# Two-layer block in fp32 pairs: shared weight buffers (7 and 4), and eight stage changes made by halves of the tokens

## The reference

```python
def rmsnorm(x, g):
    y = x * rsqrt(mean(x * x, axis=-1) + EPS)          # per token, over the 1024 channels
    return y * g

# first block, before each mixer and each FFN
h = rms_norm(x, g) * (1 + scale) + shift
x = x + gate * stage(h)                                # stage: w_in ... w_out, or gate/up/down

# second block, six times
hn = rmsnorm(x, pre_g) * (1 + scale) + shift
y = rmsnorm(fn(hn), post_g)
x = x + res_w * gate * y
```

## Time and profile before

| | us |
|---|---|
| median of 3 runs | 3777.99 (3772.76 to 3780.68) |
| the profiled execution's own time | 3780.26 |
| its span | 3778.2 |
| TensorE matmul busy | 3590.5 (95%) |
| VectorE busy | 2017.1 (53%) |
| ScalarE busy | 1333.3 (35%) |
| mean granted TensorE clock | 0.969 |
| DMA | 429.06 MB, 114 GB/s |

### The profile page before, as it was taken

How to read it: one execution, slowest core, us unless ns; L and a number is a source line. 1 busy time by engine, 2 the same in 40 slices (tenths; PEclk the granted TensorE clock), 3 DMA queues, 4 the chain that set the end, 5 groups by cost and what they waited for, 6 DMA issues and landing times.

```text
span 3778.2 us, 41003 instructions
## 1 busy us (share of the span) xinstructions
PE 3590.5 (95%) x16372; PEld 2854.7 (76%) x16372; DVE 2017.1 (53%) x3608; ACT 1333.3 (35%) x2291; POOL 127.9 (3%) x126
## 2 busy tenths in 40 slices
PE   5889999999999999998999999999999999979998
PEld 4647888766788788876677888788878888868886
DVE  7856756676766664456765235523553333344234
ACT  3563323344323332234443223322323334333232
POOL 3330000000000000000100000000000000000000
PEclk9999999989999999999999999999999999989999
DMA  6214554422455545422012222222222222212221
GB/s 250 101 40 162 191 197 165 177 80 90 163 201 184 188 178 198 154 67 75 23 51 78 100 96 95 83 96 95 101 77 83 73 79 86 66 51 95 100 95 62
DMA packets 155466, 429.06 MB, mean 114 GB/s; under 512 B 45467, under 2 KB 50523, under 8 KB 155276
## 3 DMA queue, kind: packets, MB, share of 16 engines
q1 hardware_dynamic: 155276, 426.45, 32.5%
HBM read 423.98 MB, written 2.40 MB: 113 GB/s over the span
## 4 chain that ended last, share of the span: by engine, by line
PE 83%; DVE 11%; ACT 3%; issue 1%; DMA 1%; POOL 0%; SPq 0%; ACTq 0%; DVEq 0%; POOLq 0%
PE ps L412 24%; PE ps L414 24%; PE ps L413 24%; PE ps L711 1%; PE ps L449 1%; PE ps L456 1%; DVE TT L1515 1%; DVE wlo L1448 1%; DVE HL L1500 1%; PE ps L751 1%; PE ps L789 1%; DVE X L1601 1%; PE ps L776 1%; PE ps L557 1%; PE ps L570 1%
## 5 line engine op out<-in xcount | busy, mean ns | idle before, releaser
L412 PE MATMUL ps<-HH,whi 128*128 128x512 f32 x3168 | 1262.7, 399 | 49.9 <-DVE HL L1500 27.8
L413 PE MATMUL ps<-HL,whi 128*128 128x512 f32 x3168 | 1243.8, 393 | 0.0
L414 PE MATMUL ps<-HH,wlo 128*128 128x512 f32 x3168 | 1243.6, 393 | 0.0
L1448 DVE TENSOR_TENSOR wlo<-wraw,whi 128x1024 fp32r<-128x1024 f32 x526 | 644.0, 1225 | 787.3 <-ACT whi L914 787.1
L914 ACT ACTIVATE whi<-wraw 128x1024 fp32r<-128x1024 f32 x548 | 576.3, 1054 | 697.4 <-PE ps L414 685.2
L412 PEld LDWEIGHTS ps<-HH,whi 128*128 128x128 f32 x3168 | 601.8, 190 | 207.4 <-issue 65.0
L413 PEld LDWEIGHTS ps<-HL,whi 128*128 128x128 f32 x3168 | 602.0, 190 | 127.4 <-issue 4.6
L414 PEld LDWEIGHTS ps<-HH,wlo 128*128 128x128 f32 x3168 | 601.0, 190 | 128.1
L1436 DVE CUSTOM_DVE_ANT_0 mraw<-mraw,CB 128x1024 f32<-128x1024 f32 x224 | 282.5, 1262 | 0.6 <-DMA mraw<-mst 0.5
L1634 DVE TENSOR_TENSOR TT<-TT,ps 128x512 f32<-128x512 f32 x116 | 79.7, 687 | 216.9 <-PE ps L414 187.6
L412 PE MATMUL ps<-PHf,whi 128*128 128x512 f32 x352 | 136.9, 389 | 0.0
(11 more groups left out here) (325 smaller groups left out, 3844.1 us busy)
## 6 DMA issues: line engine op xcount, KB each, us to landing
wraw<-wst SPq DMA_DIRECT2D x548, 512.0 KB, 3.7
mraw<-mst SPq DMA_DIRECT2D x224, 512.0 KB, 3.4
MR<-mst SPq DMA_DIRECT2D x16, 512.0 KB, 13.8
X<-xt SPq DMA_DIRECT2D x8, 256.0 KB, 5.1
BB<-bvec SPq DMA_DIRECT2D x8, 256.0 KB, 4.5
TT<-lse SPq DMA_DIRECT2D x16, 128.0 KB, 3.1
out<-X SPq DMA_DIRECT2D x8, 256.0 KB, 2.0
CB<-crow SPq DMA_DIRECT2D x2, 512.0 KB, 4.2
```

The lines of the kernel that those rows point to most:

```text
L412: e.matmul(o[key], wh, sh(k), start=k == 0, stop=False)
L413: e.matmul(o[key], wh, sl(k), start=False, stop=False)
L414: ins = e.matmul(o[key], wl, sh(k), start=False, stop=k == nk - 1)
L1448: e.tensor_tensor(wlo[:, x % SPLIT, :], wraw[:, x % RAW, :], whi[:, x % SPLIT, :].bitcast(F32), ALU.subtract).then_inc(*wlo_made.up(x))
```

## The change

**Buffers.** RAW is 7, SPLIT 4, and wlo has no buffer of its own: it is written over wraw of the same block. So `load(b)` waits for ("w", b - RAW) in place of the wlo of that block, and whi of a block is free one block later. SyncE's steps in `dilated()` are moved to fit, and the six first projections of mla become 4 and 2.

**Halves.** In the eight stage changes the last outputs (from m = 5 with out_proj, from 6 with a down-projection) are made first for tokens 0 to 255 and then for 256 to 511, with 256-column matmuls in a pass over the same weights each (`proj_halves`, `end_halves`); so are the first four projections (`begin_halves`). Sums, root, spread and modulation are made for each half. The sums and spread of the first half stand among the matmuls of the second pass of the outputs, those of the second half among the first pass of the projections. ("w", b) is signalled in the second pass alone. `seam` (ScalarE), `single_seam` and `double_seam` (VectorE) give the order of the rest, `fed_late` the places of the last three feeds. The norms after dilated(), the first norm and the last stay as they were.

```diff
-RAW, SPLIT = 5, 3
+RAW, SPLIT = 7, 4
...
-    gs = [(8, [("mla_in", i) for i in range(6)])]
+    gs = [(8, [("mla_in", i) for i in range(4)]), (8, [("mla_in", i) for i in (4, 5)])]
...
+        raw_off = pos[0]
         wraw = sb("wraw", [P, RAW, BT * 128])
+        wlo = at("wlo", raw_off, [P, RAW, BT * 128], F32R)
         whi = sb("whi", [P, SPLIT, BT * 128], F32R)
-        wlo = sb("wlo", [P, SPLIT, BT * 128], F32R)
...
+        split_at = {("f", 0, 1): 5, ("f", 1, 0): 6, ("f", 1, 1): 5, ("p", 0, 0): 6,
+                    ("q", 0, 0): 6, ("q", 0, 1): 5, ("q", 0, 2): 6, ("q", 1, 0): 6}
...
+            def proj_halves(order, nk, sh, sl, ready, apart, hook):
+                first = lane.tile
+                for hf in (0, 1):
+                    lane.tile = first
+                    cs = slice(256 * hf, 256 * hf + 256)
+                    for n, (key, k) in enumerate(order):
+                        wh, wl, names = weights(1)
+                        own = key + (hf,) if apart else key
+                        if k == 0 and (apart or hf == 0):
+                            take(own, apart[hf] if apart else main[0])
+                        o = ps[:, bank_of[own], cs]
+                        lane.wait_ge(*ready(k, hf))
+                        e.matmul(o, wh, sh(k)[:, cs], start=k == 0, stop=False, skip_group_check=True)
+                        e.matmul(o, wh, sl(k)[:, cs], start=False, stop=False, skip_group_check=True)
+                        ins = e.matmul(o, wl, sh(k)[:, cs], start=False, stop=k == nk - 1, skip_group_check=True)
+                        up = names if hf else []
+                        if k == nk - 1:
+                            up = up + ([own] if apart else []) + ([key] if hf else [])
+                        if up:
+                            ins.then_inc(*mm_done.up(*up))
+                        hook(hf, n)
...
+            def end_halves(s, keys, nk, sh, sl, ready):
+                sa, order = halves_of(s)[0], [(key, k) for key in keys for k in range(nk)]
+
+                def hook(hf, n):
+                    if hf and n == (5 if s[0] == "q" else 4):
+                        half_total(sa)
+                    elif hf and n == (len(order) - 1 if s[0] == "q" else 11):
+                        half_spread(sa)
+
+                proj_halves(order, nk, sh, sl, lambda k, hf: ready(k), (Ring(0, 1, 2), Ring(*((3, 0, 7) if len(keys) == 3 else (2, 7)))),
...
+
+                def hook(hf, n):
+                    if not hf and n == 7:
+                        half_total(sb)
+                    elif not hf and n == 23:
+                        half_spread(sb)
+
+                main[0] = Ring(0, 1, 2, 3)
+                proj_halves([(key, k) for k in range(8) for key in keys], 8, hh, hl, lambda k, hf: (v_norm, ("hl", z + (hf,), k)), None,
+                            hook)
...
+            def modulate_half(s, v, last_read, beside):
...
+                for m in range(8):
+                    lane.wait_ge(v_norm, ("b", s, m))
+                    e.activation(HH[:, m, cs], T[m % 5][:, cs], ACT.Identity, bias=MOD[:, v, m:m + 1]).then_inc(
+                        *a_norm.up(("hh", s, m)))
+                    beside(m)
+
+            def fed_late(m):
+                if m in (3, 5, 7):
+                    feed(8)
+
...
+            def modulate_half(s, v, idx, beside, prior=None, update=None):
...
+                for m in range(8):
+                    if m >= 5:
+                        lane.wait_ge(v_norm, ("hl", s, m - 5))
+                    if update is not None:
+                        lane.wait_ge(v_norm, ("x", prior, m))
+                    e.scalar_tensor_tensor(T[m % 5][:, cs], X[:, m, cs], AM[:, idx, m:m + 1], R, ALU.mult, ALU.mult).then_inc(
+                        *v_norm.up(("b", s, m)))
+                    if update is not None and m < 7:
+                        update(m + 1)
+                    if update is not None:
+                        lowered(m)
+                    elif m:
+                        lowered(m - 1)
+                    beside(m)
+                if update is None:
+                    lowered(7)
...
+            def single_seam(s, key, gate, nk):
...
+                square_add(s, first - 1)
+                if nk == 8:
+                    feed(8)
+                for m in range(first, 8):
+                    update(sa, m)
+                single(sa)
+                feed(nk)
+                for m in range(first, 7):
+                    update(sb, m)
+
+                def beside(m):
+                    if m == 0:
+                        feed(nk)
+                    elif m == 3:
+                        update(sb, 7)
+                        feed(8)
+                    elif m == 5:
+                        single_half(sb)
+                    elif m == 6:
+                        single_root(sb)
+
+                modulate_half(sa, v, idx, beside)
+                modulate_half(sb, v, idx, fed_late)
...
+            def double_seam(s, stage, nk):
...
+                square_add(s, first - 1)
+                gained_add(s, first - 1)
+                if nk == 8:
+                    feed(8)
+                for m in range(first, 8):
+                    output(sa, m)
+                first_half(sa)
+                roots(sa)
+                feed(nk)
+                for m in range(first, 7):
+                    output(sb, m)
+                rsqrt(za, 4)
+                diagonal(za, 4, T[2])
+
+                def beside(m):
+                    if m == 0:
+                        feed(nk)
+                    elif m == 1:
+                        output(sb, 7)
+                    elif m == 2:
+                        first_half(sb)
+                    elif m == 3:
+                        roots(sb)
+                    elif m == 4:
+                        feed(8)
+                    elif m == 5:
+                        rsqrt(zb, 4)
+                        diagonal(zb, 4, T[2])
+
+                modulate_half(za, v, nxt, beside, sa, updater(sa))
+                modulate_half(zb, v, nxt, fed_late, sb, updater(sb))
...
             def load(b):
                 if b < nblocks:
                     if b >= RAW:
-                        lane.wait_ge(lo_signal(b - RAW), b - RAW)
+                        lane.wait_ge(mm_done, ("w", b - RAW))
...
                     for n in range(9):
-                        if c < 7 or n < 4:
+                        if c < 7 or 5 <= n < 8:
                             feed(8)
-                        if n == 1 and c:
-                            totals(c - 1)
-                        elif n == 2 and c:
+                        if n == 2 and c:
                             inverses(c - 1)
-                        elif n == 5:
+                        elif n == 3:
                             maxima(c)
-                        elif n == 6:
+                        elif n == 4:
                             tops(c)
-                totals(7)
+                        elif n == 8:
+                            totals(c)
                 inverses(7)
```

More of the change, by code:

```diff
@@ L402, in weights @@
                 last = o + n == BT or lane.tile == len(tiles)
-                return whi[:, b % SPLIT, sl], wlo[:, b % SPLIT, sl], [("w", b)] if last else []
+                return whi[:, b % SPLIT, sl], wlo[:, b % RAW, sl], [("w", b)] if last else []
             def proj(keys, nk, sh, sl, ready, between=None, ks=None):
@@ L464, in norm_total, with half_sums @@
                 spread(s, next_bank)
[L466 to L470, removed]
+            def half_sums(s, o, src, rhs, at_, first=False):
+                for j in range(2 * s[3], 2 * s[3] + 2):
+                    ins = e.matmul(o[:, 4 * j + at_:4 * j + at_ + rhs.shape[1]], src[:, 128 * j:128 * j + 128], rhs,
+                                   start=first and j == 2 * s[3], stop=j == 2 * s[3] + 1, skip_group_check=True)
+                return ins
@@ new lines, in half_spread @@
+            def half_spread(s):
+                o = take(("root", s), Ring(4 + s[3]))
+                for at_, r in ((0, s), (256, after(s) if s[0] == "q" else None)):
+                    if r is not None:
+                        root_at[r], bank_of[("root", r)] = at_, bank_of[("root", s)]
+                        lane.wait_ge(v_norm, ("dg", r))
+                        e.matmul(o[:, at_:at_ + 256], C["ones"][:], (T[0] if r[0] == "q" else T[2])[:, tokens(r)], start=True,
+                                 stop=True, skip_group_check=True).then_inc(*mm_done.up(("root", r)))
@@ L516, in out_proj @@
+            def out_proj(stage, sh, sl, ready, behind):
+                main[0] = Ring(*range(8))
+                for m in range(split_at[behind]):
                     proj([("o", stage, m)], 8, sh, sl, ready)
+                end_halves(behind, [("o", stage, m) for m in range(split_at[behind], 8)], 8, sh, sl, ready)
             ev_norms = Ring(2, 3)
@@ new lines, in of_output, with square_of @@
```

(20 more changed lines are left out.)

355 lines of the change are left out of this document (243 added, 112 removed).

## The result

The changed kernel takes 3848.6 us (median of 4 runs, 3847.9 to 3852.3) where the one before takes 3779.3 in the same comparison: ratio 1.0185, 95% interval 1.0172 to 1.0197, so **+69 us**. The forecast was 3820 (+42), inside a range to 3856: slower, as forecast, but by 27 us more (the kernel before took 3778.0 in the runs that the forecast started from).

The account below looks back on a forecast made before the run. TensorE was taken as the bound (busy 3590.5 of 3778.2 us). 3780.3 + 23.6 (single changes) + 24.7 (double changes) - 6 (fourth buffer) = 3822.6, or 3820 against the median; range 3790 to 3856.

Parts of the forecast that it names:

- the largest term: Single changes' second projection pass: feeds behind m = 3, 5, 7 wait for TensorE's own progress; 19.6 us for 11.5.
- full clock in the second pass: Single changes' second pass: matmuls between stalls run 0.12 us apart, 1.43 us per k, the pass 19.6 us.
- half clock in the stalls: Rival: new 3 to 4 us idles bring back the lower clock in some loops; 20 us, 3840; chance 0.15.
- Double changes: Four stage changes with a second norm: 59.9 us against 53.0 to 53.5, 61.2 against 56.2 after mla; together +24.7.
- VectorE's own work binds: Double changes' projection passes: VectorE needs 1.64 us per m and half, 3.3 for both halves against 2.7 now.
- The half matmul: TensorE in stage changes: a 256-column matmul starts every 0.120 us, a pair 0.239 for 0.227; +16 us over 1314 replaced.
- Covered feeds: Rival: second-pass feeds find whi made, TensorE binds single changes, -30 us for four, double some -4; 3738; chance 0.13.
- Costed at nothing: Seven loads ahead, SyncE's moved steps in dilated(), changed bank rings and mla's split projections: taken as costing nothing.
- Late loads: Rival: the shared buffer holds SyncE back, whi waits for its DMA; 2 us at each change, 3836; chance 0.05.
- the even case: Rival: stalls half as long as worked out, 118 us of loss only redistributed; 3778; chance 0.05.
- The fourth buffer: Kernel start: SPLIT 4 lets whi(3) be made earlier, removing 5.9 us idle; 6.8 us earlier on TensorE, about 6 passed on.
- own range: Whole kernel: half operations at 0.34 or 0.475 us on some 380 give -19 and +32, so 3798 to 3850.

Follow-up runs that it names:

- the filled run: Changed kernel plus 12 unused 512-column matmuls in each of TensorE's three idles in single changes' second passes; 3836.1 us, ratio 1.0153 to the kernel before.
- late feeds: Changed kernel with the second pass's three feeds moved from behind m = 3, 5, 7 to behind the last HL; 3792.0 us, ratio 1.0034 to the kernel before.
- The filled kernels: Unused matmuls in TensorE's waits: changed kernel, single changes, 3836.1 us; kernel without residual addition, feeds moved last, double changes' first passes, 3775.5 us (oversized filling 3820.2).

## Why the prediction was right, and where it was short

**Slower, by the largest term: shown.** "That feed waits for whi(B4), which needs the buffer of B0" is what the rows have, and moving the feeds alone gave 57 us back, 47 of them in the single changes. The idles ahead of k = 3, 5, 7 were given as about 3 us; they are 2.97, 2.86 and 1.45 in the first change, 2.97, 2.04 and 2.58 in the second. The first pass was put at 14.7 and measured at 14.5 to 15.4, the idle ahead of it at 4.1 and measured at 3.1 to 4.6, the second half of the outputs at 10.1 and 9.95.

**The step that was short: full clock in the second pass.** The hand timeline ran the matmuls between the stalls at 0.12 us and gave 19.6 for the pass; it is 22.2 to 23.2. The term is the k behind each stall, 1.43 us in the forecast's turn of 5.7: it took 3.02 at half clock and 1.79 at full. The case *half clock in the stalls* stood in the list at 0.15 with 20 us in all, 3840. It did occur, in the single changes: with 3 us idles 23.2 at 0.78, with the same idles filled 20.8 at 1.00, without them 11.5 at 1.00. It didn't occur in the second pass of the double ones, whose idles are 0.9 to 1.5 us (clock 1.00). The ground for the low chance was that the trace had shown the lower level only after 5.9 and 9.9 us of idle, and that reading was wrong. The 9.9 us of the earlier trace rows are no single idle: between 339.79 and 349.26 TensorE made the one-column sums and the spread, and its longest wait was 2.56; the spread itself, behind a wait of 2.32, already took 2.04 us, at half clock. Two windows of the kernel before show it (the granted clock is the third number from the right): the first over that stretch, the second around a wait of 2.93 us and the k behind it, whose first matmul stands below:

```profile
341.00:349.50 8.50, 3.33 (x11) 1.74 (x12) 3.68 (x11) 2.54 (x6) 0.00 (x0) 0.65 0.24 93
...
48.00:52.00 4.00, 3.04 (x12) 2.17 (x12) 3.93 (x9) 0.66 (x2) 0.00 (x0) 1.00 0.00 0
...
48.41 0.50 PE L412 MATMUL ps<-HH,whi 128*128 128x512 f32 x1 [2.93 <-DVE HL L2149]
```

So the trace at hand had waits of 2.3 to 2.9 us with either level behind them, and both prices belonged in the sum. The single changes carry 15.6 us of the miss (239.2 for 223.6 forecast), 13.3 of it in their second passes; of these the filled run gives 8.3 back (9.5 with the first passes, 12.5 in the time). Of the other 5.0 us 3.0 are the 0.37 that the forecast left out of each of the eight turns.

**Double changes: right to 1 us at full clock, 8.7 us short in sum.** Forecast 59.9; the one that ran at full clock throughout took 60.4, with 22.2 and 15.8 us for the passes where 21.1 and 16.4 were worked out. The step of 1.64 us per m is in the rows. VectorE's timeline there, one m from Ya to Ya:

```profile
2441.16 0.47 DVE L1900 SCALAR_TENSOR_TENSOR Ya<-Ya,GM,ps 128x256 f32<-128x256 f32 x1
2441.67 0.42 DVE L1903 TENSOR_TENSOR X<-X,Ya 128x256 f32<-128x256 f32 x1
2442.01 0.48 DVE L1714 SCALAR_TENSOR_TENSOR HL<-TT,MOD,HH 128x256 fp32r<-128x256 f32 x1
2442.41 0.47 DVE L1727 SCALAR_TENSOR_TENSOR TT<-X,AM,ps 128x256 f32<-128x256 f32 x1
2442.80 0.47 DVE L1900 SCALAR_TENSOR_TENSOR Ya<-Ya,GM,ps 128x256 f32<-128x256 f32 x1
```

From one Ya to the next 1.64, a b or HL 0.39 to 0.40, the update 0.85. Where the clock was 0.73, TensorE held VectorE up by its sums (a wait of 3.9 us in place of 0.8): 25.3 us for the pass, 64.6 for the change. "VectorE's own work binds" holds at full clock, and there with only 1.3 us of room in the first pass: ScalarE's HH, TensorE's sums and a half-clocked TensorE stand close behind. Of the terms, the feeds at k = 3, 5, 7 cost the double changes 3.0 us each too.

**The half matmul: right.** 0.12 us apart (TensorE's starts at 2436.80, 2436.92, 2437.03 in the changed kernel, at full clock), so 96 in 11.5 us. By the formula of the Trainium skill (TensorE: Matmul & The Clock Gate, Back-to-back issue gap) 96 would take 10.5 us; the four passes of 11.5 to 11.6 us with late feeds, TensorE busy throughout, show 10% more, as the earlier trace rows did. That section adds that its formula is for a matmul by itself and under-counts at small widths, where each brings a weight load; each does here; the forecast left that half of the rule out.

**Covered feeds, the faster rival: half true.** Nothing covers the feeds where the change has put them. Behind the last step they are covered, and then the halves do gain at a single change, 0.7 to 3.6 us each; the 7.5 us that the rival gave each supposed that the wait of 3 to 4.6 us ahead of the first projection would go too, and it only moved.

**Costed at nothing: right, as far as tested.** The loads and the moved steps of `dilated()` cost nothing measurable, since the buffers alone are 3 us faster. The changed bank rings and mla's 4 and 2 projections are in no run by themselves; outside the stage changes the changed kernel is 4 us shorter than the one before, which leaves little room for them. Late loads (whi waits 4.3 us for its DMA in the whole changed kernel) and the even case didn't come about.

**The fourth buffer: half the size.** The idle of 5.9 us at 60 is gone, but ahead of the k before it one of 2.8 us (0.96 in the kernel before), waiting for HL, has come, and half clock behind it as before. Taken at the same matmul of the kernel before, the changed one is 5.7 us ahead at 94 and 6.9 at 113 to 126, as forecast (6.8); then 2.1 at 173, none (0.4 behind) at 214 to 285, and 1.3 at 295. Between 126 and 214 TensorE waits 17.1 us for 13.9 before, most of it for ScalarE (12.7 for 10.8); that accounts for 3 of the 7 us, the rest isn't shown. Forecast 6, measured 3 with the buffers alone.

**Sum.** In the spans the changed kernel is 26 us over the forecast (68.4 for 42.3). The stage changes are 24.3 us over it and the start gave 4.7 less; some 3 us that the rest of the kernel gained stay unexplained, as do 1 to 6 us in the experiments between the changes' lengths in a trace and the medians; single executions of the kernel before lie up to 12 us apart, its medians within 2. The time lies in the upper part of the stated range, which had been drawn with the clock case in mind. The narrower own range of 3798 to 3850 doesn't follow from its -19 and +32, which give 3801 to 3852.

## What to carry to other kernels

When two passes share one set of weights, the buffers come free only in the second; a step that feeds the next weights must then stand behind everything that the second pass waits for, or it closes a loop in which each engine waits for the other. Before an idle of some us is priced by its length, the matmuls behind it are to be priced at both clock levels, first of all those that lie on the loop, and the higher price taken where the rows show either level behind so short an idle. And what looks like one long idle is to be looked through for the work inside it. Splitting a stage change pays only where the helper engines have time left for the second set of instructions: here yes with one norm (46 to 50 us for 50, with the late feeds), no with two (57 to 60 for 53 to 56).

## What was not expected of the hardware

Three idles in a pass, the first of 3.0 us and the others of 1.5 to 3.0, with 3 to 6 us of matmuls between them, brought its granted clock to 0.78 to 0.86 (mean, in the changed kernel and in the one with the halves at single changes alone), where three idles of 0.9 to 1.5 us left it at 1.00. In the first pass of the double changes one and the same stream of instructions got 0.72 in one place and 1.00 in another of the same run, and 24.1 or 20.9 us by it; with work that nobody uses, 0.44 us after each k, all four took 21.3. The filled kernels are faster for more matmuls: 12.5 us at single changes, 5 to 6 us at double ones. And a matmul on float32 constants took 0.22 us for 128 columns, where one on the kernel's rounded operands takes 0.12 for 256.
